# Turning queries and probabilities by DMA instead of TensorE in the second mixing stage of a two-block transformer kernel

## What is computed

```python
def diff_attention(q, k, v, q_g, k_g, rel_bias, lam, subln_g, lambda_init):
    q = rmsnorm_2(q, q_g)
    k = rmsnorm_2(k, k_g)
    ...
        logits = jnp.einsum('bqhcd,bkhcd->bhcqk', q_blk, k).astype(jnp.float32) * scale
        logits = logits + bias[None, :, None]
        logits = jnp.where(rel >= 0, logits, -jnp.inf)
        p = jax.nn.softmax(logits, axis=-1)
        attn = p[:, :, 0] - lam * p[:, :, 1]
        return jnp.einsum('bhqk,bkhe->bqhe', attn.astype(v.dtype), v)
    ...
    out = rmsnorm_2(out, subln_g) * (1.0 - lambda_init)
```

## Time and profile before

| | us |
|---|---|
| median of 3 runs | 997.86 |
| lowest, highest | 997.59, 997.95 |
| profiled execution | 998.35 |
| its span, first to last instruction | 996.5 |
| TensorE busy in it | 990.7 |
| VectorE busy | 689.2 |
| ScalarE busy | 548.2 |
| GpSimd busy | 116.0 |

### The profile page before, as it was taken

The page is one execution under the profiler, slowest core; times in us unless marked ns, Lnnn a source line. Parts: engine busy times, 40 slices in busy tenths (PEclk is TensorE's granted clock), DMA queues, the critical chain, the costliest instruction groups (busy, mean ns, idle before and its releaser), DMA issues.

```text
span 996.5 us, 12586 instructions
## 1 busy us (share of the span) xinstructions
PE 990.7 (99%) x4632; PEld 813.2 (82%) x4632; DVE 689.2 (69%) x1010; ACT 548.2 (55%) x752; POOL 116.0 (12%) x109
## 2 busy tenths in 40 slices
PE   8999999999999999999999999999999999999998
PEld 7788888888877788888888888888888888888887
DVE  6756566668987667656566677797689767656663
ACT  7344443576765546444443576768875555443542
POOL 0000000022300000000000041168914000000000
DMA  7987776585444446666666376457556546787761
GB/s 258 283 262 258 234 253 211 185 307 175 147 150 141 169 133 211 227 204 208 220 195 226 127 259 211 141 177 211 148 183 199 205 152 212 227 221 227 223 199 43
DMA packets 159129, 199.87 MB, mean 201 GB/s; under 512 B 49633, under 2 KB 105322, under 8 KB 158954
## 3 DMA queue, kind: packets, MB, share of 16 engines
q1 hardware_dynamic: 159066, 199.24, 62.8%
q10 hardware_dynamic: 16, 0.00, 0.0%
HBM read 182.45 MB, written 5.77 MB: 189 GB/s over the span
## 4 chain that ended last, share of the span: by engine, by line
PE 97%; DVE 1%; DMA 1%; ACT 0%; SPq 0%; issue 0%; POOL 0%; ACTq 0%; DVEq 0%; POOLq 0%
PE bank L1902 23%; PE bank L1904 23%; PE bank L1903 23%; PE bank L2018 7%; PE bank L2019 7%; PE bank L2020 7%; PE bank L1917 1%; PE bank L2069 1%; PE bank L2183 1%; DMA halves_t<-halves 0%; DMA raw<-in_ffn_w_gu 0%; PE bank L2084 0%; PE bank L2071 0%; PE bank L2257 0%; PE bank L2141 0%; PE bank L2304 0%
## 5 line engine op out<-in xcount | busy, mean ns | idle before, releaser
L1902 PE MATMUL bank<-hi,xh 128*128 128x512 f32 (+1 forms) x944 | 375.2, 397 | 0.9 <-DVE lo L1520 0.8
L1904 PE MATMUL bank<-hi,xl 128*128 128x512 f32 (+1 forms) x944 | 367.4, 389 | 0.0
L1903 PE MATMUL bank<-lo,xh 128*128 128x512 f32 (+1 forms) x944 | 366.5, 388 | 0.0
L1277 DVE TENSOR_TENSOR lo<-raw,hi 128x2048 fp32r<-128x2048 f32 (+1 forms) x111 | 253.9, 2289 | 146.3 <-ACT hi L799 146.3
L799 ACT ACTIVATE hi<-raw 128x2048 fp32r<-128x2048 f32 (+1 forms) x114 | 216.5, 1901 | 132.3 <-PE bank L2020 96.9
L1902 PEld LDWEIGHTS bank<-hi,xh 128*128 128x128 f32 x944 | 177.3, 188 | 39.5 <-issue 3.1
L1904 PEld LDWEIGHTS bank<-hi,xl 128*128 128x128 f32 x944 | 177.2, 188 | 37.5
L1903 PEld LDWEIGHTS bank<-lo,xh 128*128 128x128 f32 x944 | 177.6, 188 | 34.2
L1294 DVE TENSOR_TENSOR lo<-raw,hi 128x1024 fp32r<-128x1024 f32 (+1 forms) x108 | 133.2, 1244 | 40.1 <-ACT hi L808 39.2
L2018 PE MATMUL bank<-hi,hh 128*128 128x512 f32 (+1 forms) x306 | 119.3, 390 | 0.4 <-DVE hl L1353 0.4
L2020 PE MATMUL bank<-hi,hl 128*128 128x512 f32 (+1 forms) x306 | 118.7, 388 | 0.0
(11 more groups left out here) (266 smaller groups left out, 963.2 us busy)
## 6 DMA issues: line engine op xcount, KB each, us to landing
raw<-in_w_in SPq DMA_DIRECT2D x48, 1024.0 KB
raw<-in_ffn_w_gu SPq DMA_DIRECT2D x82, 512.0 KB
raw<-in_ffn_w_down SPq DMA_DIRECT2D x22, 1024.0 KB
raw<-in_w_up SPq DMA_DIRECT2D x16, 1024.0 KB
raw<-in_w_down SPq DMA_DIRECT2D x16, 1024.0 KB
raw<-in_w_out SPq DMA_DIRECT2D x8, 1024.0 KB
distance_table<-ftab SPq DMA_DIRECT2D x8, 576.0 KB
raw<-in_w_proj_attn SPq DMA_DIRECT2D x4, 1024.0 KB
```

The source lines that it names most:

```text
L1277: nc.vector.tensor_tensor(lo[s][:, :, 0:width], raw[s][:, :, 0:width], hi[s][:, :, 0:width].bitcast(F32), ALU.subtract).then_inc(lo_done, 1)
L1902: nc.tensor.matmul(o, sh, wh, start=first and j == 0, stop=False)
L1903: nc.tensor.matmul(o, sh, wl, start=False, stop=False)
L1904: ins = nc.tensor.matmul(o, sl, wh, start=False, stop=last and j == 3)
```

## The change

- The queries (groups 0 and 3) are no longer turned by TensorE. ScalarE makes planes of `hid` (passes 4, 5, 16, 17), SyncE issues two DMA turns for each group, VectorE merges them into `q_2` in passes 7 and 20. The planes lie in `rg` and `grt`, which are free then. The keys are turned as before; their gain column now holds the product of both gains.
- The combined probabilities are no longer turned by TensorE. ScalarE makes planes (128x768 halves) in pass second entry + 3, SyncE issues one DMA turn, VectorE merges into `pt2` in pass second entry + 5, and the value block stands behind portion second entry + 6. Planes and turned planes lie in the head's own buffer `l2`.
- Combining is done with one scaling less: the first pair is not scaled, and the factor of the first sum goes into the eviction of the values, which becomes two instructions.
- ScalarE issues the four lambda loads, in its pass 0, instead of SyncE.
- The counts that other waits compare with follow from this.

The core of the diff:

```diff
@@ -103,8 +103,13 @@
-M2_T = {(c, t): 4 * (c + 1) + 1 + t for c in (0, 1, 3, 4, 5, 7, 8, 9) for t in range(NT)}
+M2_T = {(c, t): 4 * (c + 1) + 1 + t for c in (1, 4, 5, 7, 8, 9) for t in range(NT)}
 M2_STEP = [12, 13, 15, 16, 18, 19, 21, 22, 24, 25, 26, 27, 29, 30, 32, 33]
+M2_PLANES = {4: (0, 0), 5: (0, 1), 16: (3, 0), 17: (3, 1)}
+M2_MERGE = {7: 0, 20: 3}
+M2_P_PLANES = [p + 3 for p in M2_STEP[1::2]]
+M2_P_MERGE = [p + 5 for p in M2_STEP[1::2]]
+M2_PV = [p + 6 for p in M2_STEP[1::2]]
...
@@ -647,18 +670,32 @@
+            def flip_queries(c):
+                for t in range(NT):
+                    sp_eng.wait_ge(ffns[1].planes, 2 * (NF1 - 1) + 2 * (c // 3) + t + 1)
+                    sp_eng.dma_start_transpose(q_turned_planes_of(c)[:, :, t * P:(t + 1) * P],
+                                               q_planes_of(c)[:, t, :]).then_inc(ffns[1].flip[t], 16)
+            def flip_probabilities(h):
+                sp_eng.wait_ge(k_pt, h + 1)
+                if h >= 2:
+                    sp_eng.wait_ge(k_ptc, h - 1)
+                sp_eng.dma_start_transpose(p_turned_planes_of(h), p_planes_of(h)).then_inc(ffns[0].flip[h % 2], 16)
             for c, (first, _) in enumerate(IN2):
                 for half in range(2):
                     if half == 1 and by_dma(c - 3):
                         flip_mixed(c - 3)
                     columns(a["w_in_2"], U_M2 + 2 * c + half, first, half)
-                if c == 1:
-
+                    for h in range(NH):
+                        if 2 * c + half == (M2_P_PLANES[h] - 1) // 2 + 5:
+                            flip_probabilities(h)
+                if c in (3, 6):
+                    flip_queries(c - 3)
+                if c == 2:
                     sp_eng.wait_ge(n_sq, 8)
-                    for j, name in enumerate(("lambda_q1_2", "lambda_k1_2", "lambda_q2_2", "lambda_k2_2")):
-                        vector = a[name].rearrange("a n -> (a n)")
-                        sp_eng.dma_start(lamv[:, j, :], vector.partition_broadcast(P)).then_inc(lam_in, 16)
-                if c == 2:
...
@@ -1121,6 +1158,17 @@
                 rstd = rstd_x[:, t:t + 1]
+                if p == 0:
+                    for j, name in enumerate(("lambda_q1_2", "lambda_k1_2", "lambda_q2_2", "lambda_k2_2")):
+                        vector = a[name].rearrange("a n -> (a n)")
+                        act.dma_start(lamv[:, j, :], vector.partition_broadcast(P)).then_inc(lam_in, 16)
+                if p in M2_PLANES:
+                    cc, tt = M2_PLANES[p]
+                    act.wait_ge(k_qn, 4 * (cc // 3) + tt + 1)
+                    nc.scalar.activation(q_planes_of(cc)[:, tt, :].rearrange("p (s c) -> p s c", s=2),
+                                         hid[:, tt, :].bitcast(U16).rearrange("p (c s) -> p s c", s=2),
+                                         ACT.Copy).then_inc(ffns[1].planes, 1)
...
@@ -1128,27 +1176,27 @@
                 key = key_at(M2_T, p)
-                if key is not None and not by_dma(key[0]):
+                if key is not None and key[0] in (1, 4):
                     cc, tt = key
-                    order = list(M2_T).index(key)
-                    act.wait_ge(k_tr, order + 1)
+                    if key == (1, 0):
+                        act.wait_ge(cols_done, 5)
+                    act.wait_ge(k_tr, 2 * (cc // 3) + tt + 1)
                     view = X[0][:, :].rearrange("p (k c) -> p k c", c=P)
                     rows = slice(tt * P, (tt + 1) * P)
-                    dst = q_2 if cc in (0, 3) else k_2
-                    g = C_GAIN + (4 if cc in (0, 3) else 5)
-                    nc.scalar.activation(dst[:, 4 * (cc // 3):4 * (cc // 3) + 4, rows], view, ACT.Copy,
-                                         scale=cols[:, g:g + 1]).then_inc(k_trev, 1)
+                    nc.scalar.activation(k_2[:, 4 * (cc // 3):4 * (cc // 3) + 4, rows], view, ACT.Copy,
+                                         scale=cols[:, C_GAIN + 5:C_GAIN + 6]).then_inc(k_trev, 1)
                 for h in range(NH):
-                    if M2_STEP[2 * h + 1] + 4 == p:
-                        act.wait_ge(k_pt, h + 1)
-                        if h >= 2:
-                            act.wait_ge(k_pv, h - 1)
-                        nc.scalar.activation(pt2[:, h % 2, :], PT[:, 0:SPAN], ACT.Copy).then_inc(k_ptc, 1)
-                    if M2_STEP[2 * h + 1] + 5 == p:
+                    if M2_P_PLANES[h] == p:
+                        act.wait_ge(k_comb, h + 1)
+                        nc.scalar.activation(p_planes_of(h).rearrange("p (s c) -> p s c", s=2),
+                                             l2[:, 0, h % 3, :].bitcast(U16).rearrange("p (c s) -> p s c", s=2),
+                                             ACT.Copy).then_inc(k_pt, 1)
+                    if M2_PV[h] == p:
                         act.wait_ge(k_pv, h + 1)
-                        nc.scalar.activation(xn[:, :, h * P:(h + 1) * P],
-                                             O[h % 2][:, 0:SEQ].rearrange("p (t c) -> p t c", t=NT),
-                                             ACT.Copy).then_inc(k_oev, 1)
+                        for tt, o in ((1, O[h % 2][:, P:SEQ]), (0, O[h % 2][:, 0:P])):
+                            ins = nc.scalar.activation(xn[:, tt, h * P:(h + 1) * P], o, ACT.Copy,
+                                                       scale=inv[:, 4 * h + 1 - tt:4 * h + 2 - tt])
+                        ins.then_inc(k_oev, 1)
...
@@ -1158,8 +1206,10 @@
                         m = 2 * (0, 1, 3, 4).index(c) + t
-                        if m >= 2:
-                            act.wait_ge(k_tr, m - 1)
+                        if c == 3:
+                            act.wait_ge(k_tr, t + 1)
+                        if c in (1, 4):
+                            act.wait_ge(ffns[1].planes, 2 * (NF1 - 1) + 2 * (c // 3) + t + 1)
...
@@ -1753,15 +1807,13 @@
                         c1 = inv[:, 4 * h + 2:4 * h + 4]
-                        step(nc.vector.tensor_scalar(c1, c1, lam[:, 4:5], None, ALU.mult))
-                        for q, s in enumerate((slice(0, SEQ), slice(SEQ, SPAN))):
-                            one = l2[:, 1, h % 3, s]
-                            ins = nc.vector.tensor_scalar(one, one, inv[:, 4 * h + 2 + q:4 * h + 3 + q], None, ALU.mult)
-                            ins = ins if q == 0 else step(ins)
+                        step(nc.vector.scalar_tensor_tensor(c1, c1, lam[:, 4:5], sums[:, 4 * h:4 * h + 2],
+                                                            ALU.mult, ALU.mult))
                         for q, s in enumerate((slice(0, SEQ), slice(SEQ, SPAN))):
                             zero = l2[:, 0, h % 3, s]
-                            ins = nc.vector.scalar_tensor_tensor(zero, zero, inv[:, 4 * h + q:4 * h + q + 1],
-                                                                 l2[:, 1, h % 3, s], ALU.mult, ALU.add)
+                            ins = nc.vector.scalar_tensor_tensor(zero, l2[:, 1, h % 3, s],
+                                                                 inv[:, 4 * h + 2 + q:4 * h + 3 + q],
+                                                                 zero, ALU.mult, ALU.add)
...
@@ -1796,6 +1848,22 @@
                                                    ALU.mult, ALU.subtract).then_inc(k_ol, 1)
+                h = at(M2_P_MERGE, p)
+                if h >= 0:
+                    dve.wait_ge(ffns[0].flip[h % 2], 16 * (NF1 - 1) + 16 * (h // 2) + 16)
+                    if h >= 2:
+                        dve.wait_ge(k_pv, h - 1)
+                    nc.vector.tensor_copy(pt2[:, h % 2, :].bitcast(U16).rearrange("p (k c s) -> p s k c", c=P, s=2),
+                                          p_turned_planes_of(h).rearrange("p (s k) c -> p s k c", s=2)
+                                          ).then_inc(k_ptc, 1)
+                if p in M2_MERGE:
+                    cc = M2_MERGE[p]
+                    for tt in range(NT):
+                        dve.wait_ge(ffns[1].flip[tt], 16 * (NF1 - 1) + 16 * (cc // 3) + 16)
+                    dst = q_2[:, 4 * (cc // 3):4 * (cc // 3) + 4, :]
+                    nc.vector.tensor_copy(dst.bitcast(U16).rearrange("p k (c s) -> p s k c", s=2),
+                                          q_turned_planes_of(cc).rearrange("p (s k) c -> p s k c", s=2)
+                                          ).then_inc(ffns[1].merged, 1)
...
@@ -2261,23 +2329,17 @@
                     if k == 0:
-                        pe.wait_ge(k_trev, 4)
+                        pe.wait_ge(k_trev, 2)
+                        pe.wait_ge(ffns[1].merged, NF1)
                         pe.wait_ge(res_done, 12)
                     else:
                         pe.wait_ge(k_l, k)
                     if k == NH:
-                        pe.wait_ge(k_trev, 8)
+                        pe.wait_ge(k_trev, 4)
+                        pe.wait_ge(ffns[1].merged, NF1 + 1)
                     pair_scores(q_2, h, k_2, h, k_s)
                 for h in range(NH):
```

(10 more changed lines are left out.)

26 lines of the change are left out of this document (20 added, 6 removed).

## The result

| | before | changed |
|---|---|---|
| median, us | 997.86 | 1007.23 |
| lowest, highest | 997.31, 998.02 | 1006.70, 1007.39 |
| profiled execution | 998.35 | 1006.83 |
| its span | 996.5 | 1005.0 |

The ratio is 1.0093, with a 95% interval of 1.0082 to 1.0104: the changed kernel is slower, by 9.37 us in the medians and by 8.48 between the two profiled executions. The forecast was 1003.6, +5.7. The direction came as forecast and the size is 1.6 times as large; the median lies 0.4 us above the forecast's own range of 1000.2 to 1006.8, and inside the wider one that ends at 1008.

What follows compares the result with a forecast made beforehand. TensorE, busy for 990.7 of 996.5 us, was taken to bound the kernel. From the median 997.86, -4.1 us of its stream and +9.8 of waits net +5.7, giving 1003.6 us, range 1000.2 to 1006.8.

Steps and rivals of the forecast that it cites:

- the wider one: Range for the whole kernel's time, 995.5 to 1008 us, leaving out 0.2 of the chances in all.
- The bound: Second mixing stage: TensorE waits for nothing, so work leaving its stream comes off and added waits come on, one for one.
- TensorE's stream, -4.1 us: TensorE in the stage: removed query blocks 1.83 and probability turns 2.68, less 0.39 for three tails coming back.
- The race at the value blocks, +9.8: Value blocks: TensorE waits for VectorE's merges at seven heads, 9.8 us in sum, 3.1 at head 0.
- own lateness: VectorE's delay in reaching a readable score block: 1.3 us at head 2, 1.15 at head 5.
- The clock: TensorE in the stage: clock column read as 1.00, the 2.4 GHz level; no term for a drop.
- The DMA turns are hidden: Query and probability turns: landing 2.3 us after issue, 8.2 at worst, taken as adding no time.
- the reserve of up to 2 us: First query merge: if its flips take 8.2 us behind a weight unit, up to 2 us is added.
- The lambda loads, 0, at most 0.3: Loads moved from SyncE to ScalarE's issue slots while it waits for the norm: cost 0, at most 0.3 us.
- The rivals: Four alternatives: race won 0.15, only half the waits 0.15, flips late too 0.13, change moves nothing 0.01.
- rival 1: Value blocks: VectorE and ScalarE run ahead, only 1.5 us of waiting stays, 995.3 us; chance 0.15.
- Rival 3: SyncE's queue: flips come late, two query merges and two heads each 1.5 us later, 1009.6 us; chance 0.13.

Runs made afterwards that it cites:

- the best kernel: Changed kernel with every step of the query and probability chains asked for later (value blocks + 8 instead of + 6): 993.59 us, ratio 0.9955.
- two experiments: Changed kernel with second query group's planes one pass later, 1004.23 us; changed kernel with 12 extra matmuls before head 0's value-block wait, 1006.69 us.

## Why the prediction was right or wrong

**The bound.** Right. What leaves TensorE comes off, what makes it wait comes on: in the kernel with all steps later TensorE waits for nothing in the stage and the time is 4.5 below the kernel before.

**TensorE's stream, -4.1 us.** Right. In the best kernel the stage is 4.4 us shorter, and in the changed one the stream is 4.5 shorter by difference. Some 0.3 of either is not the stream but the gap at portion 8, which went with the lambda loads; that leaves 4.1 and 4.2. By the Trainium skill's 390 ns for a 128x128 bf16 turn on TensorE (VectorE: DVE Perf Modes, "The three transpose paths") the estimate for 40 turns was 15.6 us. That is not seen here: 4.5 is the most that any kernel gained.

**The race at the value blocks, +9.8.** Right in kind, in place and nearly in size: 10.5, and 0.6 more for getting under way six times. Expected were seven waits that the merge ends, the longest at head 0 and the next at head 5; there are six.

| head | predicted | distance from the last matmul |
|---|---|---|
| 0 | 3.1 | 3.0 |
| 1 | 1.0 | 0 |
| 2 | 1.0 | 1.7 |
| 3 | 0.9 | 1.1 |
| 4 | 1.0 | 1.8 |
| 5 | 2.1 | 1.5 |
| 6 | 0.7 | 1.4 |
| sum | 9.8 | 10.5 |

Head 1 has no wait because the slow clock had delayed TensorE; without the drop it waits 1.0, as two experiments show. That the sum comes within 8% is in part luck: head 1 and head 5 were put 1.6 too high together, heads 2, 4 and 6 2.2 too low. For head 0 the chain went step by step as worked out, the idle time of ScalarE included, which reads 2.37 us where about 2 was predicted:

```profile
618.42 1.06 ACT L1169 ACTIVATE grt<-hid 128x1024 uint16<-128x1024 uint16 x1 [2.37 <-DVE hid L1650]
619.38 0.83 ACT L1191 ACTIVATE l<-l 128x768 uint16<-128x768 uint16 x1
...
623.77 1.04 ACT L845 ACTIVATE hi<-raw 128x1024 fp32r<-128x1024 f32 x1
```

For heads 2, 4 and 6 the waits were about 0.7 us longer each. The term that was off is VectorE's "own lateness", which I took over from the kernel before. For head 2 it was 1.3. In the changed kernel the score block starts at 648.04 and could be read at 648.99; VectorE came 2.0 later, behind a lo split that waited for ScalarE:

```profile
648.74 1.05 ACT L845 ACTIVATE hi<-raw 128x1024 fp32r<-128x1024 f32 x1
649.82 1.22 DVE L1344 TENSOR_TENSOR lo<-raw,hi 128x1024 fp32r<-128x1024 f32 x1 [2.11 <-ACT hi L845]
650.97 0.42 DVE L1516 CUSTOM_DVE_ANT_0 l<-bank,bias 128x256 f32<-128x256 f32 x1
```

ScalarE had been busy without a gap since it read head 1's values at 642.70, and those stand one portion later than before. So the likely cause is that ScalarE's hi splits are now tied to the later value blocks; no run isolates it. It is not that one wait makes the next: with head 0's wait 2.3 us shorter and head 1's back, in the kernel with the planes of the second query group later, head 2's is the same, 1.5:

```profile
650.94 0.38 PE L2352 MATMUL bank<-v,pt 128*128 128x128 f32 x1 [1.53 <-DVE pt L1856]
```

VectorE was not full at head 6, as the prediction had it; it stood waiting for ScalarE ahead of that combining:

```profile
689.56 1.23 DVE L1344 TENSOR_TENSOR lo<-raw,hi 128x1024 fp32r<-128x1024 f32 x1 [1.18 <-ACT hi L845]
```

Head 5 was too high because its lateness was 0.9, not 1.15, and combining took 2.0, not 2.35. One name in the working is wrong, without effect on its numbers: the score block in front of a merge (646.03 for head 2, 674.08 for head 5) is that of head h+2, and what VectorE combines behind its logits is head h+1.

**The clock.** The step that failed outright. "The clock column says 1.00, the 2.4 GHz level" was read from a kernel in which TensorE has no such wait in the stage, and kept for one in which I predicted a wait of 3.1 us. It cost 1.6 us on TensorE; with what it covered at head 1 the time would be 0.5 lower without it. Even so it is the largest single term that was missing. With the waits (1.3 more than 9.8) and the key turn (0.56, which had no term) it makes up the 3 us or so by which the stage exceeds the forecast.

**The DMA turns are hidden.** Right at the value blocks; at the first query merge the reserve of up to 2 us was used with 0.5. That VectorE would meet a transfer there was expected; what stands behind the merge in its list (the scaling of keys) was not worked out.

**The lambda loads, 0, at most 0.3.** At its bound for the step from one kernel to the other: their move takes a gap of 0.3 us out of TensorE's stream, which I had overlooked in the kernel before. Wrong as a general price: it is worth about 3 us in the changed kernel, where TensorE comes to stand behind the turns that they delay. The forecast doesn't suffer from that, since the changed kernel has the better place.

**The rivals.** None came true. The race could have been won, but not as rival 1 had it, by engines that run ahead; it takes later due times. Rival 3, late flips, has its part at the key turn only.

## What to carry to other kernels

When a step moves from one engine to a chain of several, ask at which pass each link is due, not only how long it takes: in order-bound lists an instruction that waits for something made in the pass just before stalls all that is queued behind it, and the same work asked for a pass later was 13.6 us faster. Price a wait of TensorE not only by its length but by the matmuls after it: here waits of 2.3 us and more were followed by a slow clock, and those up to 1.7 were not. And a queue entry costs what the one behind it is waited for, which the change itself may alter.

## What the runs showed of the hardware

- Three waits of TensorE, 2.86 us in the changed kernel and 2.32 and 2.86 with the lambda loads back on SyncE, were each followed by a granted clock of 0.50 for 3.4 us, with a step of 0.43 us instead of 0.23. It fell 0.1 to 1.3 us after TensorE had resumed. Waits of 0.92 to 1.65 us in the same kernels left it at 1.00, and so did dummy matmuls in place of the 2.86. The Trainium skill (TensorE: Matmul & The Clock Gate, "HAM oscillation — how this bites in real kernels") describes a kernel whose waits for DMA data make TensorE's next matmuls start at the low clock. The trace agrees that the low clock follows a wait, here one for VectorE; but at 629.30 and 633.09 us the first matmuls behind it still ran at the full one.
- In the changed kernel a DMA turn of 128x768 halves landed 2.5 us after its issue, and 4.9 to 5.5 where a weight unit had been issued at most 1.3 us before it.
- Four turns of 128x128 words cost TensorE 0.36 us start to start in a stream of matmuls, both before and after.
